# Longer rows in the split weight panels, chosen start addresses for TensorE's operands, and 528 tokens cut at 256 instead of 272

## The reference, cut to what matters

```python
# first block, twice                       # second block: 16 meta tokens + 512
h = rms_norm(x, pre_norm_g[l])             # layer 0: even mixer, layer 1: odd mixer
proj = h @ w_in[l]        # 1024 -> 3328   hn = rmsnorm(h, norm_mix[l])
... two kinds of attention ...             h = h + mixer(hn, ...)   # w_in 1024 -> 5192 / 3072, w_out 1536 / 1024 -> 1024
y = concat([ya, yb]) @ w_out[l]            hf = rmsnorm(h, norm_ffn[l])
x = x + rms_norm(y, post_norm_g[l])        u, g = hf @ w_up, causal_conv3(hf @ w_gate) + b      # 1024 -> 2816
                                           h = h + (silu(g) * u) @ w_down                       # 2816 -> 1024
```

## Time and profile before

| | |
|---|---|
| runs | 2315.2, 2318.0, 2322.7 us (median 2318.0) |
| profiled execution | span 2310.5 us from its first to its last instruction; its own total is not listed, so 7.5 us is taken for what lies around the span (median less span) |
| instructions | 35487, of them 14840 matmuls |
| TensorE's mean granted clock | 0.982 of 2.4 GHz |
| DMA | 175.64 MB, mean 76 GB/s |

### The profile page before, as it was taken

How to read it: one execution, slowest core, us unless ns; L and a number is a source line. 1 busy time by engine, 2 the same in 40 slices (tenths; PEclk the granted TensorE clock), 3 DMA queues, 4 the chain that set the end, 5 groups by cost and what they waited for, 6 DMA issues and landing times. The chain is left out here.

```text
span 2310.5 us, 35487 instructions
## 1 busy us (share of the span) xinstructions
PE 2222.1 (96%) x14840; PEld 1977.2 (86%) x14840; DVE 1123.9 (49%) x1684; ACT 965.8 (42%) x1404; POOL 621.7 (27%) x480
## 2 busy tenths in 40 slices
PE   8999999998999999998999999999999989999998
PEld 6887579885589987886899999998989989988987
DVE  3448535557452234886444424444555544433443
ACT  4346634356544335335433313334555534322332
POOL 2112320113214334346123302322333212310321
PEclk8999999999999989989999999999999999999999
DMA  6341023310123202130233233232111013323322
GB/s 192 124 150 48 0 74 102 95 51 6 40 76 92 89 31 79 56 106 1 69 105 92 70 106 92 81 91 77 37 55 56 19 55 92 93 85 106 92 81 74
DMA packets 235315, 175.64 MB, mean 76 GB/s; under 512 B 7704, under 2 KB 230160, under 8 KB 234644
## 3 DMA queue, kind: packets, MB, share of 16 engines
q1 hardware_dynamic: 234836, 173.20, 25.1%
q10 hardware_dynamic: 320, 0.17, 0.0%
HBM read 171.20 MB, written 10.09 MB: 78 GB/s over the span
## 5 line engine op out<-in xcount | busy, mean ns | idle before, releaser
L336 DVE TENSOR_TENSOR panel_lo<-panel_raw,panel_hi 128x2048 fp32r<-128x2048 f32 (+2 forms) x148 | 326.1, 2204 | 254.2 <-ACT panel_hi L328 254.1
L328 ACT ACTIVATE panel_hi<-panel_raw 128x2048 fp32r<-128x2048 f32 (+2 forms) x150 | 266.4, 1776 | 371.1 <-PE product L434 256.9
L434 PE MATMUL product<-scaled_hi,panel_hi 128*128 128x272 f32 (+2 forms) x1232 | 282.4, 299 | 2.6 <-PEq L490 1.4
L434 PE MATMUL product<-scaled_lo,panel_hi 128*128 128x272 f32 (+2 forms) x1232 | 282.9, 299 | 0.0
L434 PE MATMUL product<-scaled_hi,panel_lo 128*128 128x272 f32 (+2 forms) x1232 | 282.7, 299 | 0.0
L434 PEld LDWEIGHTS product<-scaled_hi,panel_hi 128*128 128x128 f32 x1232 | 196.5, 188 | 11.8 <-issue 3.0
L434 PEld LDWEIGHTS product<-scaled_hi,panel_lo 128*128 128x128 f32 x1232 | 195.4, 188 | 7.5
L434 PEld LDWEIGHTS product<-scaled_lo,panel_hi 128*128 128x128 f32 x1232 | 194.5, 188 | 6.7
L447 PE MATMUL product_banks<-panel_hi,scaled_hi 128*128 128x256 f32 x696 | 193.4, 278 | 0.0
L447 PE MATMUL product_banks<-panel_lo,scaled_hi 128*128 128x256 f32 x696 | 193.4, 278 | 0.0
L447 PE MATMUL product_banks<-panel_hi,scaled_lo 128*128 128x256 f32 x696 | 193.3, 278 | 0.0
(11 more groups left out here) (595 smaller groups left out, 5433.0 us busy)
## 6 DMA issues: line engine op xcount, KB each, us to landing
panel_raw<-in_w_in_dram SPq DMA_DIRECT2D x26, 1024.0 KB, 5.4
panel_raw<-in_ffn_w_gate_dram SPq DMA_DIRECT2D x44, 512.0 KB, 4.0
panel_raw<-in_ffn_w_up_dram SPq DMA_DIRECT2D x44, 512.0 KB, 5.3
panel_raw<-in_ffn_w_down_dram SPq DMA_DIRECT2D x32, 704.0 KB, 4.7
panel_raw<-in_even_w_in_dram SPq DMA_DIRECT2D x21, 1024.0 KB, 5.2
panel_raw<-in_odd_w_in_dram SPq DMA_DIRECT2D x12, 1024.0 KB, 5.1
panel_raw<-in_w_out_dram SPq DMA_DIRECT2D x8, 1024.0 KB, 6.7
panel_raw<-in_even_w_out_dram SPq DMA_DIRECT2D x8, 768.0 KB, 5.1
```

Source lines behind the costliest of these rows:

```text
L328: act.activation(c.hi[g % 2][:, 0:used], c.raw[g % 2][:, 0:used], ACT.Copy).then_inc(c.hi_made.sem, 1)
L336: dve.tensor_tensor(c.lo[g % 2][:, 0:used], c.raw[g % 2][:, 0:used], c.hi[g % 2][:, 0:used].bitcast(F32), ALU.subtract).then_inc(c.lo_made ...
L434: done = pe.matmul(banks[b], weight(w, k), a[:, k, u:v], start=(k == 0 and x == 0), stop=(k == chunks - 1 and x == 2))
```

## The change

`Product` gets a `step`: with `step=16` (64 bytes) the rows of `panel_hi` and `panel_lo` are 16 columns longer than the columns used; `panel_raw` keeps its packed rows. So ScalarE's, VectorE's and GpSimd's panel instructions write 8, 11 or 12 rows with gaps. `step=16` for the even mixer's output product, both odd products, both feed-forward in-products and the down product of feed-forward 0; `step=0` for the first block, the even mixer's in-products and the last down product. `sb` gets a `phase`: the tile's start modulo 256. `FRONT` becomes 256. To make room, `conv` moves into `norm.squares`, the third `relu` buffer into `even_total`, and a fifth of `v[0]` into the constant square's tables. No instruction is added or taken away.

```diff
-FRONT = 272
+FRONT = 256
+STEP = 16
+SLOT = PANEL + KD * STEP
+PHASE_UNIT = 256
+PANEL_PHASE = 0
+SCALED_PHASES = {0: 64, 1: 64, 4: 64, 5: 64, 6: 192, 7: 192}   # by gain: first block 0, 1; even 4; odd 5; feed-forward 6, 7
+Y_PHASES = (0, 0)
+EVEN_Y_PHASE, QUERY_PHASE = 192, 192
+INNER_PHASES = (192, 0)
...
+        size = 4 * math.prod(shape[1:])
+        if phase is not None:
+            short = (nc.sbuf_top - size - phase if side == "right" else phase - nc.sbuf_base) % PHASE_UNIT
+            if short >= ROW_UNIT:
+                into.enter_context(nc.sbuf_tensor(own("phase_pad"), [P, short // ROW_UNIT * ROW_UNIT // 4], F32, side=side))
...
-    c.hi = [sb(f"panel_hi{j}", [P, PANEL], F32R) for j in range(2)]
+    c.hi = [sb(f"panel_hi{j}", [P, SLOT], F32R, phase=PANEL_PHASE) for j in range(2)]
...
-        act.activation(c.hi[g % 2][:, 0:used], c.raw[g % 2][:, 0:used], ACT.Copy).then_inc(c.hi_made.sem, 1)
+        act.activation(panel_view(c.hi[g % 2], product), raw_view(c.raw[g % 2], product), ACT.Copy).then_inc(c.hi_made.sem, 1)
...
+        self.pitch = cols + step
...
+def raw_view(slot_tile, product):
+    return slot_tile[:, 0:product.chunks * product.cols].rearrange("p (k n) -> p k n", k=product.chunks)
 def panel_view(slot_tile, product):
-    return slot_tile[:, 0:product.chunks * product.cols].rearrange("p (k n) -> p k n", k=product.chunks)
+    rows = slot_tile[:, 0:product.chunks * product.pitch].rearrange("p (k n) -> p k n", k=product.chunks)
+    return rows[:, :, 0:product.cols]
...
-        self.relu = [*spare, c.sb("index_relu", [P, TOK], side="right", into=stage)[:]]
+        self.relu = [*spare, total[:, 0:TOK]]
...
-    out = Product(c, 12, P, [Segment(8, columns(w_out, 0, P), [("T", lambda w, k: w[:, k, :])], add_to_h(c, 1))])
+    out = Product(c, 12, P, [Segment(8, columns(w_out, 0, P), [("T", lambda w, k: w[:, k, :])], add_to_h(c, 1))], step=STEP)
...
-        v = [c.sb(f"v{j}", [P, NB2, 256], into=stage) for j in range(2)]
+        v_room = [c.sb(f"v{j}", [P, NB2 - 1 + j, 256], into=stage) for j in range(2)]
+        v = [[room[:, t, :] for t in range(NB2 - 1 + j)] for j, room in enumerate(v_room)]
+        v[0].append(c.square[:, 1:3, :].rearrange("p a n -> p (a n)"))
...
+        products.append(Product(c, KD, 256, [Segment(FF_HALF, load_inner, T_tiles(), None)], dmas=2, step=STEP))
+        products.append(Product(c, FF_HALF, P, [Segment(KD, load_down, [("T", lambda w, k: w[:, k, :])], None)],
+                                step=0 if layer else STEP))
...
-        conv = [c.sb(f"conv{j}", [P, width], into=stage) for j in range(2)]
+        conv = [t[:, 0:width] for t in norm.squares]
```

More of the change, by code:

```diff
@@ L163, in open_core @@
     c.raw = [sb(f"panel_raw{j}", [P, PANEL]) for j in range(2)]
-    c.hi = [sb(f"panel_hi{j}", [P, PANEL], F32R) for j in range(2)]
-    c.lo = [sb(f"panel_lo{j}", [P, PANEL], F32R) for j in range(2)]
+    c.hi = [sb(f"panel_hi{j}", [P, SLOT], F32R, phase=PANEL_PHASE) for j in range(2)]
+    c.lo = [sb(f"panel_lo{j}", [P, SLOT], F32R, phase=PANEL_PHASE) for j in range(2)]
     c.landed = [count(f"panel_landed{j}") for j in range(2)]
@@ L315, in load @@
             sp.wait_ge(self.c.lo_made.sem, COUNT_START + g - 1)
-        for out, src in seg.load(panel_view(self.c.raw[g % 2], product), i):
+        for out, src in seg.load(raw_view(self.c.raw[g % 2], product), i):
             sp.dma_start(out, src).then_inc(self.c.landed[g % 2].sem, 16)
@@ L2120, in first_layer @@
         with ExitStack() as stage:
-            y_parts = [c.sb(f"y_{n}", [P, KD, SEQ], F32R, into=stage) for n in ("hi", "lo")]
+            y_parts = [c.sb(f"y_{n}", [P, KD, SEQ], F32R, into=stage, phase=Y_PHASES[layer]) for n in ("hi", "lo")]
             heads_stage(c, layer, lam_init, cell, y, y_parts, heads_out, out, turn)
@@ L2665, with __init__ @@
     ROUNDS_BEFORE = {6: 1, 7: 1, 8: 1, 9: 2, 10: 1, 11: 1, 12: 2, 13: 3, 18: 2}
-    def __init__(self, c, stage, cell, score, best, spare, first_sliding):
+    def __init__(self, c, stage, cell, score, best, spare, first_sliding, total):
         self.first_sliding = first_sliding
@@ L3165, in even_layer @@
                     cell.iw = c.sb("iw", [P, NB2, 8], side="right", into=index)
-                    led_product_stage(c, selected, c.hT, TOK, 4, split, None, IndexSide(c, index, cell, score, best, spare, first_sliding), opened=True,
+                    led_product_stage(c, selected, c.hT, TOK, 4, split, None, IndexSide(c, index, cell, score, best, spare, first_sliding, total), opened=True,
                                       total=total, summed=True)
@@ L3172, in even_layer @@
             with ExitStack() as stage:
-                parts = [c.sb(f"y_{n}", [P, 12, TOK], F32R, into=stage) for n in ("hi", "lo")]
+                parts = [c.sb(f"y_{n}", [P, 12, TOK], F32R, into=stage, phase=EVEN_Y_PHASE) for n in ("hi", "lo")]
                 ahead = ahead_of_ffn(c, ahead_stage, 0)
@@ L3188, in odd_products @@
             segments.append(Segment(1, columns(w_in, 1024 * third + 256 * group, 256), tiles, None))
-    into = Product(c, KD, 256, segments)
-    out = Product(c, KD, 256, [Segment(4, columns(w_out, 0, 256), T_tiles(), add_to_h(c, 2))])
+    into = Product(c, KD, 256, segments, step=STEP)
+    out = Product(c, KD, 256, [Segment(4, columns(w_out, 0, 256), T_tiles(), add_to_h(c, 2))], step=STEP)
     return into, out
@@ L3695, in odd_layer @@
     with ExitStack() as layer:
-        q = [c.sb(f"q_{part}", [P, KD, TOK], F32R, into=layer) for part in ("hi", "lo")]
+        q = [c.sb(f"q_{part}", [P, KD, TOK], F32R, into=layer, phase=QUERY_PHASE) for part in ("hi", "lo")]
         odd_stage(c, into, q, taken, ahead)
@@ L3842, in __init__ @@
         self.c, self.src, self.gain, self.tokens, self.pending = c, src, gain, tokens, 0
-        self.hi, self.lo = (c.sb(f"scaled_{n}", [P, KD, room or tokens], F32R, side, into=stage) for n in ("hi", "lo"))
+        self.hi, self.lo = (c.sb(f"scaled_{n}", [P, KD, room or tokens], F32R, side, into=stage, phase=SCALED_PHASES.get(gain))
+                            for n in ("hi", "lo"))
     def act_hi(self, act, k):
@@ L3958, in ffn_layer @@
             ahead.behind(1)
[L3959 removed]
+        hi, lo = (c.sb(f"inner_{n}", [P, FF_HALF, width], F32R, into=stage, phase=INNER_PHASES[layer])
+                  for n in ("hi", "lo"))
         gated = [c.sb(f"gate{j}", [P, width + 2], into=stage) for j in range(2)]
[L3961 removed]
+        conv = [t[:, 0:width] for t in norm.squares]
         raised = [norm.total[:, 0:width], c.sb("raised1", [P, width], into=stage)[:]]
```

34 lines of the change are left out of this document (14 added, 20 removed).

## The result

The changed kernel takes 2305.26 us (median of 6 runs, 2300.45 to 2310.66) against 2316.36 us before (6 runs, 2315.2 to 2322.7) on the same chip: ratio 0.9949, with a 95% interval of 0.9934 to 0.9964. So it is faster by 11 us, not by 31. The profiled execution had 2309.54 us and a span of 2307.8, near the upper end of its runs; the granted clock is as in the earlier trace rows but for one slice of the 40, which has 8 tenths for 9.

What follows compares the result with a forecast made beforehand. TensorE's matmul pace was taken as the bound, with hardly any wait to remove. Parts 1 to 5 summed to 40.8 us; three quarters, 31 us, off the median of 2318.0 gave 2287 us, range 2266 to 2311.

Steps and rivals of the forecast that it cites:

- part 1: T tiles to distance 192 in feed-forward 0, even and odd output products and feed-forward 1's gate: 25.8 us gained.
- Part 2: 512-column tiles to distance 0 in the last up and down products: 2.7 and 2.5 us gained.
- Part 3: First block: in-product T tiles gain 2.0 us, N tiles 4.0 us.
- That stretch: First block, 45 to 74.9 us: N tiles already at 113.4 ns a matmul at the same distance 64.
- Part 4: Selected product: 3.7 us on TensorE, 1.2 taken because the attention waits for VectorE's ranking.
- Part 5: Odd in-product: N and T matmuls 2.3 + 3.0 us, half taken, 2.6 us.
- Part 6: Panel splits writing rows with gaps on ScalarE and VectorE: zero, upper end a few us at stage openings.
- Part 7: Aliased buffers, v[0] and FRONT alone: zero, or a us or two either way in an attention stage.
- rival 1: T tiles don't share the N tiles' taste and keep their average; only parts 2 to 5 remain: 2307 us, chance 0.21.
- Rival 2: Addresses don't matter; the stretches differ for another reason, such as DMA or other engines: 2318 us, chance 0.09.
- Rival 3: Slower: T tiles locked on a bad distance, 6.5 ns more for each of 5184 matmuls: 2346 us, chance 0.09.
- Rival 4: T tiles reach the lower end of their records, 10 ns less each: 2255 us, chance 0.04.

Runs made afterwards that it cites:

- e2: The changed kernel run once more, unchanged: 2300.25 us.
- e1: The kernel before run once more, unchanged: 2313.82 us.
- e11: Changed kernel with most 272-column matmuls cut to 256, leaving out part of 16 tokens' sums, and the selected product's scaled at 192: 2288.10 us, one run.
- e6: Changed kernel with all activations beginning at 192 (odd in-product left): 2315.05 us, one run.
- e9: Changed kernel with distance steady at every chunk where memory allows (576-token rows, selected scaled at 192): 2303.07 us, ratio to before 0.9940.
- e8: Changed kernel with the cut back at 272, longer rows and new places kept: 2312.40 us, ratio to before 0.9978.
- e10: The changed kernel again, unchanged, beside the steady version: 2306.16 us, ratio to before 0.9947.
- e12: Kernel before with only the cut at 256 instead of 272, rows and places as before: 2315.86 us, ratio 1.0001.
- e3: Changed kernel with all activations beginning at 0 (odd layer left): 2316.97 us, ratio to before 0.9996.
- e4: Changed kernel with all activations beginning at 128: 2326.58 us, ratio to before 1.0044.

## Why the prediction was right and wrong

Faster came out, and 2305 lies inside the range near its upper end, but the predicted time was 18 us too low: 31 us off the kernel before were forecast, 11 came. The term that was mis-sized is **part 1**, *T tiles to distance 192*, and in it the price borrowed from the retention's N tile. Measured are 120.8 in feed-forward 0 where 116.8 was forecast. Its parts, in surplus times count from before to after:

- feed-forward 0: 36.9 to 34.3 us, 2.6 gained for 15.5; even out 0.9 for 3.3; odd out 0.5 (0.3 by its kept steps alone) for 1.9; feed-forward 1's gate 0.2 for 5.1. Together 4.2 us for 25.8. With 4.2 in the sum it is 19.2 us, three quarters of it 14.4: part 1 makes 16 of the 20 us that the gain fell short. The rest fits what was seen above, that not all of a faster pace arrives: e2's span is 13.5 us below e1's for 18.3 us less surplus.
- Why the borrowed price did not hold: it was the low one of two rates (e1, e2, e11), taken for the rate of a place because one profile had it over 120 us. A T tile of 272 + 256 columns at a wholly steady 192 never came below 10.0 ns on average (e6, e9), between the two and nearer the dearer. And the claim of one distance was wrong at each chunk's end: the weights loaded beside a chunk's last matmul are the next chunk's, 64 bytes on, so that one matmul in six stood at 128. Made steady, the down product went from 10.8 to 10.0 (e9).
- The range of +6.5 and -10 ns a matmul, read from the spread of the records, was far too wide: the rows alone (e8) lost 1.2 ns, the whole gained 0.9.

**Part 2** was nearly right. The down product gained 234.0 - 226.9 = 7.1 ns by the counts, 6.6 by the surplus: 3.5 us for 2.5. The up product gained 0.3 for 2.7. Its panel and token rows step alike, but at each chunk's end the next weights lie 64 bytes on, beside one matmul in three; e9, where no row steps, gives 1.9 us more. With 20.0 ns for that one matmul in three (distance 192) and 13.4 for the others the mean would be 15.6; measured are 17.7, and what makes the rest is not shown. The kernel before from 2245 to 2290 us, beside the 200 matmuls of the kernel after in the first fence of stretches:

```profile
2245.00:2290.00 45.00, 45.00 (x194) 1.00 0.23 64
```

**Part 3:** 3.0 us for 6.0 in this profile, 6.9 in e2 and e10, 0.8 of each in the output product. The text put the output product at 64 in both kernels; the change puts it at 0, where it takes 30 / 132.3 = 226.8 ns for 228.5. "That stretch also warns: the distance is not the whole story" was right, and should have gone further: the two rates at one distance, 113.4 and 117.9 in the first block's N tiles, stood in the earlier trace rows, and the retention's 113.3 was the same low rate. Nothing was reserved for its going to the other, 5.4 us here.

**Part 4** gained 1.4 us for 1.2, nearly all on the N tiles (12.0 to 6.7 ns). **Part 5** gained 0.6 for 2.6: its T tiles 0.7, its N tiles nothing. **Part 6** was zero, as said. **Part 7** held for the alias buffers, but of FRONT it says too little: alone it is zero (e12), with the longer rows it is worth 2.0 ns a matmul in feed-forward 0 (e8).

The 7.5 us taken for what lies around the span were mostly something else: the other executions have 1.7 to 1.9 us there (2309.54 less 2307.8 in the kernel after), so the profiled execution of the kernel before was some 6 us faster than its median.

Of the rivals, **rival 1** gave 2307 and came nearest, for nearly its reason: T tiles keep about their average. Its "taste" is what e11 corrects: a T tile of 256 columns at a steady distance has the N tiles' two rates. **Rival 2** is refuted by e3 and e4 and by the last down product, the same 13.4 or 20.0 ns in every profile of the same place. Beside it stood the Trainium skill (SBUF — State Buffer, Who interferes with whom): two independent read ports for TensorE, and no waiting. These runs do not agree: moved only in address, the last down product takes 226.9 or 234.0 ns a matmul at full clock. Rival 2's row, 113.4 against 117.9 at one distance, was a true sign of something else beside the address, though not of the DMA or the other engines: the rate holds over 1183 matmuls while they come and go. **Rival 3**'s mechanism exists (e8, 12.8 ns), and the cut is what avoids it. **Rival 4** fails: 0.9 ns was gained, not 10.

Open: what picks one of the two rates. Granted clock, code and addresses are the same. It is set where a row of matmuls begins: in the retention it changes only at a break, and in e11's T tiles only at a tile's start. What sets it there is not shown. It comes where the distance is 64 or 192 (and, 10.7 or 12.0, in N tiles at distance 160). Why the streams' distance costs anything is argued from the pattern (with starts moved alone, the pace moves, and equal distances from other starts give equal rates), and the meeting of the two reads in SBUF is not shown as its mechanism.

## What to carry to other kernels

When the busiest engine has no waits left, count its instructions per microsecond stretch by stretch: differences at one clock and one shape are real time, and the operands' starts modulo 256 bytes are worth trying as a free parameter, for each kind of tile separately and with row steps that keep the distance. Take a second profile of the unchanged kernel before borrowing a rate from a stretch: a rate that one execution holds over 1000 matmuls may be one of two. And don't read what can be gained from the spread of record lengths; it went here from 14 to 9 ns in one group and from 11 to 15 in another, and the pace moved by under 1%.

## What the runs showed that was not expected

- The surplus comes in steps: 6.7 ns for 256 columns and 13.4 for 512 are both 1/16 over the columns' time at 2.4 GHz, and no product kept a lower surplus in any run.
- Two rates for the same instructions at the same addresses, 6.7 and 11.1 ns for 256 columns, 15.6 and 20.0 for 512. In twelve profiles with the retention at 192 or 64, seven kept the low rate over all 1183 matmuls behind the break and five the high one.
- The best place for a moving operand of 512 columns (0, 13.4 ns) is among the worst for 256 columns in N tiles (13.3 ns).
- Writing panel rows with 64-byte gaps cost ScalarE nothing and VectorE 2% (1915 and 2426 ns for 2048 elements).
